# Local attention heads: scores from split queries and keys instead of float32 products, and an output projection whose first products wait row tile by row tile

## The reference, cut to what matters

```python
def swa_sinks_attention(q, k, v, sinks):       # q: 8 heads, k, v: 2 key heads, of 64 columns each
    ...                                        # keys of the block before and of the own block
    scores = jnp.einsum('bnqkgd,bnskd->bnkgqs', qb, kb).astype(jnp.float32) * scale
    scores = scores + alibi[None, None]
    scores = jnp.where(valid[None, :, None, None], scores, -jnp.inf)
    ...
    out = jnp.einsum('bnkgqs,bnskd->bnqkgd', p, vb)

mixed = jnp.concatenate([out_a.reshape(b, s, A_Q_W), out_b.reshape(b, s, B_W)], axis=-1)
x = x + jnp.einsum('bse,ed->bsd', mixed, w_out)
```

## Time and profile before

| | us |
|---|---|
| runs | 2723.07, 2725.77, 2720.76; median 2723.07 |
| profiled execution, its own time | 2724.15 |
| its span in the trace | 2722.3 |
| PE busy in the span | 2633.6 (97%) |
| DVE / ACT / POOL busy | 1837.4 / 1326.2 / 405.3 |
| end of block 2's projections | about 1700 to 1742 |
| attention of block 2 | about 1742 to 1987 |
| output projection of block 2 | about 1989 to 2045 and on |

### The profile page before, as it was taken

How to read it: one execution, slowest core, us unless ns; L and a number is a source line. 1 busy time by engine, 2 the same in 40 slices (tenths; PEclk the granted TensorE clock), 3 DMA queues, 4 the chain that set the end, 5 groups by cost and what they waited for, 6 DMA issues and landing times. The chain is left out here.

```text
span 2722.3 us, 37072 instructions
## 1 busy us (share of the span) xinstructions
PE 2633.6 (97%) x13612; PEld 2193.7 (81%) x13612; DVE 1837.4 (67%) x2469; ACT 1326.2 (49%) x1952; POOL 405.3 (15%) x359
## 2 busy tenths in 40 slices
PE   8999999999999899999999999899999999999999
PEld 7888876877788888888888788778888788888887
DVE  5761365457524888888888857566625875857878
ACT  3111243567432577877787422555533553525353
POOL 0222212100230122222221022300020000000000
PEclk9999999999999999999999999999999999999999
DMA  3115124311452699999999332100032616253451
GB/s 128 54 47 182 40 74 131 127 39 52 137 179 109 237 378 380 386 381 371 374 371 348 139 105 68 39 1 1 1 132 66 266 49 248 71 187 135 157 183 62
DMA packets 142456, 437.83 MB, mean 161 GB/s; under 512 B 23408, under 2 KB 45680, under 8 KB 110576
## 3 DMA queue, kind: packets, MB, share of 16 engines
q1 hardware_dynamic: 125312, 402.40, 41.0%
q0 software_dynamic: 10656, 20.99, 2.2%
q10 hardware_dynamic: 6352, 12.58, 1.2%
HBM read 387.68 MB, written 66.06 MB: 167 GB/s over the span
## 5 line engine op out<-in xcount | busy, mean ns | idle before, releaser
L2729 DVE TENSOR_TENSOR w_lo<-w_raw,w_hi 128x2048 fp32r<-128x2048 f32 x192 | 437.2, 2293 | 60.3 <-ACT w_hi L2663 59.3
L2663 ACT ACTIVATE w_hi<-w_raw 128x2048 fp32r<-128x2048 f32 x187 | 355.8, 1925 | 39.5 <-PE banks L2790 39.5
L3660 PE MATMUL banks<-b_parts,a_parts 128*128 128x512 f32 x1344 | 306.9, 390 | 6.3 <-DVE a_parts L3715 6.3
L3660 PE MATMUL banks<-a_parts,b_parts 128*128 128x512 f32 x1344 | 306.0, 389 | 2.3 <-DVE a_parts L3715 1.2
L3660 PEld LDWEIGHTS banks<-b_parts,a_parts 128*128 128x128 f32 x1344 | 251.8, 188 | 60.9 <-DVE a_parts L3715 8.8
L3660 PEld LDWEIGHTS banks<-a_parts,b_parts 128*128 128x128 f32 x1344 | 252.0, 188 | 55.2 <-DVE a_parts L3715 1.6
L3689 ACT ACTIVATE b_parts<-w_quarter 128x1024 fp32r<-128x1024 f32 x112 | 118.6, 1059 | 281.4 <-PE banks L3660 266.8
L766 POOL TENSOR_TENSOR w_lo<-w_raw,w_hi 128x512 fp32r<-128x512 f32 (+2 forms) x132 | 158.6, 1207 | 576.6 <-ACT w_hi L745 575.4
L745 ACT ACTIVATE w_hi<-w_raw 128x512 fp32r<-128x512 f32 (+2 forms) x132 | 73.9, 573 | 324.0 <-PE banks L824 306.0
L3709 DVE TENSOR_TENSOR b_parts<-w_quarter,b_parts 128x1024 fp32r<-128x1024 f32 x112 | 136.9, 1222 | 132.5 <-ACT b_parts L3689 132.5
L824 PE MATMUL banks<-w_hi,act_hi 128*128 128x512 f32 (+1 forms) x576 | 219.9, 382 | 6.0 <-POOL w_lo L766 3.7
(11 more groups left out here) (545 smaller groups left out, 5560.8 us busy)
## 6 DMA issues: line engine op xcount, KB each, us to landing
w_raw<-in_w SPq DMA_DIRECT2D x192, 1024.0 KB, 7.4
a_parts<-scratch_x_parts SPq DMA_DIRECT2D x42, 1024.0 KB, 4.8
w_raw<-in_w_in SPq DMA_DIRECT2D x80, 256.0 KB, 2.7
w_quarter<-in_w_up SPq DMA_DIRECT2D x16, 1024.0 KB, 6.9
w_quarter<-in_w_down SPq DMA_DIRECT2D x16, 1024.0 KB, 8.0
scratch_x_parts<-a_parts SPq DMA_DIRECT2D x14, 1024.0 KB, 5.1
scratch_gateT<-gate_staged SPq DMA_DIRECT2D x32, 256.0 KB, 2.2
gate<-scratch_gateT SPq DMA_DIRECT2D x32, 256.0 KB, 3.6
```

The costliest lines, as they stand in the source:

```text
L2663: act.activation(hi[c % SLOTS][:, :], raw[c % TILES][:, :], ACT.Copy).then_inc(hi_done, 1)
L2729: dve.tensor_tensor(lo[c % SLOTS][:, :], raw[c % TILES][:, :], hi[c % SLOTS][:, :].bitcast(F32), ALU.subtract).then_inc(lo_done, 1)
L3660: mm = pe.matmul(out, left, right, start=(start and n == 0), stop=(stop and n == 2))
```

## The change

1. **Scores of the local heads.** `qaT[g]` becomes fp32r with all 128 partitions in use: in the half that belongs to key head g the high part of the queries, in the other half their low part. `ka_hi[g]` holds the high part of key head g in both halves, `ka_lo` the low parts, each with three places ("slots") of 128 keys. A head's scores are two products: 128 rows (queries high and low against keys high) and 64 rows (queries high against keys low).
2. **Their preparation (step 2).** ACT makes four copies instead of three. DVE, which had no work there, makes four subtractions (two of 64x512, two of 64x128). POOL, which had none either, copies `ka_hi` from the one half into the other (2 copies) and, in even row tiles, also into slot 0 for the next row tile (5 more); each of its copies waits for the one before, the seventh for DVE too. PE's `wait_prepared` now waits for ACT, DVE and POOL in step 2 as well. In `project2_stage` the transposes after tile 30 wait for DVE's part of step 2, and DVE does that part after scaling four tiles of keys. Two memsets of `qaT` go.
3. **Output projection.** The four first weight tiles are loaded and split in the prelude (`Ring`): ACT puts their high parts between its sixteen copies, POOL makes the low parts meanwhile, and PE no longer waits for all sixteen parts of the rows but, for the first weight tile, for those of each row tile.

```diff
-    OF_ACT, OF_DVE = (2, 2, AKV + 1), (2, 2, 0)
+    OF_ACT, OF_DVE, OF_POOL = (2, 2, 4), (2, 2, 4), ((2, 2, 7), (2, 2, 2))
...
+    def pool_keys(self, pool, t):
+        n, done, k = self.own_slot(t), self.pool_upto[t, 2] - self.OF_POOL[t % 2][2], self.ka_hi
+        copies = [(k[0][self.BOTTOM, n, :], k[0][self.TOP, n, :]), (k[1][self.TOP, n, :], k[1][self.BOTTOM, n, :])]
+        if t % 2 == 0:
+            for r in (self.TOP, self.BOTTOM):
+                copies += [(k[0][r, 0, :], k[0][self.TOP, n, :]), (k[1][r, 0, :], k[1][self.BOTTOM, n, :])]
+            copies.append((self.ka_lo[:, 0, :], self.ka_lo[:, n, :]))
+        pool.wait_ge(self.prep_act, self.act_upto[t, 2])
+        for i, (dst, src) in enumerate(copies):
+            if done + i:
+                pool.wait_ge(self.prep_pool, done + i)
+            if i == 6:
+                pool.wait_ge(self.prep_dve, self.dve_upto[t, 2])
+            pool.tensor_copy(dst, src.bitcast(F32)).then_inc(self.prep_pool, 1)
...
+    def dve_local(self, dve, t, banks):
+        for b, bank in enumerate(banks):
+            dve.wait_ge(self.prep_act, self.act_upto[t, 2] - 2 + 2 * b)
+            n = self.own_slot(t)
+            for g, (own, other) in enumerate(((self.TOP, self.BOTTOM), (self.BOTTOM, self.TOP))):
+                if b == 0:
+                    lo, hi, src = self.v.qaT[g][other, :, :], self.v.qaT[g][own, :, :], self.blocks(bank, own)
+                else:
+                    lo, hi, src = self.ka_lo[own, n, :], self.ka_hi[g][own, n, :], bank[own, 0:P]
+                dve.tensor_tensor(lo, src, hi.bitcast(F32), ALU.subtract).then_inc(self.prep_dve, 1)
...
     def wait_prepared(self, pe, t, step):
         pe.wait_ge(self.prep_act, self.act_upto[t, step])
-        if self.dve_upto[t, step]:
-            pe.wait_ge(self.prep_dve, self.dve_upto[t, step])
-            pe.wait_ge(self.prep_pool, self.dve_upto[t, step])
+        pe.wait_ge(self.prep_dve, self.dve_upto[t, step])
+        pe.wait_ge(self.prep_pool, self.pool_upto[t, step])
...
-                30: [turn_first(0, 0, EARLY, (ops.columns_set, 1), (ops.prep_act, ops.act_upto[0, 2]))],
+                30: [turn_first(0, 0, EARLY, (ops.columns_set, 1), *after_both(0, 2))],
...
         scale(3, "kb", range(4))
+        ops.dve_part(dve, 0, 2, EARLY)
         ops.dve_part(dve, 0, 0, EARLY)
...
                     for a in range(HALF):
-                        mm = pe.matmul(pair[:, a * u.keys:(a + 1) * u.keys], qaT[u.g][:, a, :], kaT[:, (u.i + 1) * P - u.keys:(u.i + 1) * P],
-                                       start=True, stop=True)
+                        own = pair[:, a * u.keys:(a + 1) * u.keys]
+                        pe.matmul(own, qaT[u.g][:, a, :], ops.ka_hi[u.g][:, keys, :].rearrange("p n k -> p (n k)"), start=True, stop=False)
+                        mm = pe.matmul(own, qaT[u.g][rows_, a, :], ops.ka_lo[rows_, keys, :].rearrange("p n k -> p (n k)"), start=False, stop=True)
...
+    WEIGHTS_AFTER = {3: 0, 9: 1, 13: 2, 15: 3}
...
+    def row_waits(self, t):
+        return [(self.lo_done, max(2 * t + 2, 8 + t + 1))]
...
+        for n in range(self.COUNT):
+            act.wait_ge(self.turned, n + 1)
+            act.activation(self.part(v.act_hi, n), self.turned_rows(n), ACT.Copy).then_inc(self.hi_done, 1)
+            if n in self.WEIGHTS_AFTER:
+                i = self.WEIGHTS_AFTER[n]
+                act.wait_ge(self.ring.landed[i], 16)
+                act.activation(v.w_hi[:, i, :], v.w_raw[:, i, :], ACT.Copy).then_inc(self.ring.hi_done, 1)
...
+    tiles[0].rows_ready = {t: mixed.row_waits(t) for t in range(NT)}
```

More of the change, by code:

```diff
@@ L492, in __init__ @@
         self.first, self.last, self.b0 = first, last, b0
-        self.after = None
+        self.after, self.rows_ready = None, {}
         self.units = range(*rows_) if kind == "nat" else range(2 * (cols // P))
@@ L813, in _ @@
                         pe.wait_ge(free, freed[b])
+                    for s, count in tile.rows_ready.get(u, ()):
+                        pe.wait_ge(s, count)
                     if tile.kind == "nat":
@@ L1932, in _ @@
             keep_clock(pe, v, 7, 22)
[L1936 to L1991, removed]
-                mm = pe.transpose(v.bank[n % 8][:, c * P:(c + 1) * P], chunk(t, 4 * h + c), v.ident[:, :])
-            mm.then_inc(turned, 1)
-    return Prelude(sync, scalar, vector, tensor, [(hi_done, 2 * NT), (lo_done, 2 * NT)])
 BRANCH_W = 2 * P
@@ L3132, in f @@
             ops.pool_part(pool, t, step)
-            pool.wait_ge(ops.prep_pool, ops.dve_upto[t, step])
+            pool.wait_ge(ops.prep_pool, ops.pool_upto[t, step])
         return f
@@ L3208, in dve_program @@
         dve.wait_ge(attention_in, 48)
-        for g, r in enumerate((slice(HD, P), slice(0, HD))):
-            done(dve.memset(v.qaT[g][r, :, :], 0.0))
         done(dve.memset(v.R[:, :, :, :], 0.0))
@@ L3348, in _ @@
         def _(pool):
-            for t in range(2, NT):
-                pool.wait_ge(scored, starts[t - 1])
-                for step in range(2):
-                    ops.pool_part(pool, t, step)
+            for t, step in ops.SEQUENCE[5:]:
+                if step < 2:
+                    pool.wait_ge(scored, starts[t - 1])
+                ops.pool_part(pool, t, step)
         @block.vector
@@ L3500, in _, with __init__, part, turned_rows @@
             weigh(n_units - 1)
+class MixedRows:
+    COUNT = 2 * NT
+    WEIGHTS_AFTER = {3: 0, 9: 1, 13: 2, 15: 3}
+    def __init__(self, v, ring):
+        sem = v.sem
+        self.v, self.ring = v, ring
+        self.turned, self.hi_done, self.lo_done = sem("rows_turned"), sem("rows_hi"), sem("rows_lo")
+        self.ready = [(self.lo_done, self.COUNT)]
+    def part(self, x, n):
+        t, h = divmod(n, 2)
+        return x[:, 4 * h:4 * h + 4, t * P:(t + 1) * P]
+    def turned_rows(self, n):
+        return self.v.bank[n % 8].rearrange("p (c t) -> p c t", c=4)
+    def row_waits(self, t):
+        return [(self.lo_done, max(2 * t + 2, 8 + t + 1))]
+    def scalar(self, act):
+        v = self.v
+        for n in range(self.COUNT):
[5 more added lines that the diff above has]
+                act.activation(v.w_hi[:, i, :], v.w_raw[:, i, :], ACT.Copy).then_inc(self.ring.hi_done, 1)
+    def vector(self, dve):
+        v = self.v
+        for n in range(self.COUNT):
+            dve.wait_ge(self.hi_done, n + 1)
+            dve.tensor_tensor(self.part(v.act_lo, n), self.turned_rows(n), self.part(v.act_hi, n).bitcast(F32), ALU.subtract).then_inc(self.lo_done, 1)
+    def tensor(self, pe):
+        v = self.v
+        for n in range(self.COUNT):
+            t, h = divmod(n, 2)
+            if n >= 8:
+                pe.wait_ge(self.lo_done, n - 7)
+            for c in range(4):
+                mm = pe.transpose(v.bank[n % 8][:, c * P:(c + 1) * P], (v.out_a, v.out_b)[h][:, t, c * P:(c + 1) * P], v.ident[:, :])
+            mm.then_inc(self.turned, 1)
 def output2_stage(v):
     sem, d = v.sem, v.d
-    def mixers(t, k):
-        return (v.out_a if k < 4 else v.out_b)[:, t, k % 4 * P:(k % 4 + 1) * P]
     act = (v.act_hi, v.act_lo)
@@ L3512, in output2_stage, with load_w @@
     ready, free, x_in = sem("bank_ready"), sem("bank_free"), sem("x_in")
-    prelude = turn_rows(v, mixers)
+    ring = Ring(v)
+    mixed = MixedRows(v, ring)
+    tiles[0].rows_ready = {t: mixed.row_waits(t) for t in range(NT)}
+    def load_w(sp):
+        ring.load_first(sp, tiles)
     def load_x(sp):
```

39 lines of the change are left out of this document (26 added, 13 removed).

## The result

| | before | changed |
|---|---|---|
| median of the runs, us | 2722.84 (2720.76 to 2725.77) | 2771.37 (2767.72 to 2775.86) |
| ratio | | 1.0177, interval 1.0165 to 1.0190 |
| profiled execution, its own time | 2724.15 | 2769.5 |
| its span | 2722.3 | 2767.8 |

The changed kernel is slower by 48.5 us, where +5.1 was forecast and 2738 was the upper end. The profile after, in the order of the rows of before. First the page's busy time of the engines (answers to rows 1): PE is busy 36 us longer, so most of the loss isn't a wait.

The account below looks back on a forecast made before the run. The prediction took PE, busy for 97% of the span, as the bound; -10.0 + 12.2 + 2.6 - 4.2 + 4.5 = +5.1 us on 2723.07 gave 2728.2 us, range 2715 to 2738.

Parts of the forecast that it names:

- score products: Window units in the attention: two fp32r products a head at 0.12 us each, 0.83 us less in 12 units, -10.0 us.
- waits after step 2: Attention, row tiles 1 to 7: PE waits for DVE (odd) or POOL (even) at the shared banks, +12.2 us.
- waits ahead of preparations: PE's waits ahead of the transposes that a preparation starts with in the attention; the prediction had no term for them.
- projection stage: Step 2 of row tile 0: PE's transposes after tile 30 start 1.7 us late, and POOL's low part is later, +2.6 us.
- output projection: Its start: first weights are split earlier, so PE's first product comes 2.8 us sooner and a low-clock spell goes, -4.2 us.
- the clock: Attention and projection stage: three spells of low clock after the new waits, about 1.5 us each, +4.5 us.
- the products gain nothing: Rival on the score products: a 64-row load can't be hidden behind the product before, +15 us, 2738; chance 0.03.
- no faster DVE: Rival: six low-clock spells, and DVE's projection-stage scaling no faster while POOL stands, +12 us, 2735; chance 0.17.

Follow-up runs that it names:

- e2: The changed kernel with 128 rows instead of 64 in the second product of a head too: 2731.0 us.
- e1: The kernel before with the new order of the output projection alone: 2717.5 us.
- e8: The changed kernel with 64 rows in both products of a head, the queries' low parts left out of the first: 2737.7 us.
- e5: The changed kernel with a window unit's products ordered 128, 128, 64, 64 rows, so half as many changes of row count: 2739.0 us.
- e4: The changed kernel with its whole preparation and waits, but one float32 product a head, keys' low parts left out: 2740.3 us.
- e7: e2 with the shared banks waiting for ACT and DVE only and the weighing put ahead of that wait: 2713.6 us.
- e3: The kernel before with the two products a head (128 and 64 rows) from ACT's plain copies, no low parts or new waits: 2738.8 us.
- e6: The changed kernel with the shared banks waiting for ACT and DVE only and the weighing put ahead of that wait: 2743.3 us.
- e12: The changed kernel with six unread float32 products by the identity behind each window unit's scores from row tile 1 on: 2769.3 us.
- e11: The changed kernel with six unread float32 products by the identity in each wait behind step 2 from row tile 2 on: 2762.6 us.

## Why the prediction was wrong

The terms in the prediction's order; measured in the changed kernel unless said otherwise.

| term | forecast | measured |
|---|---|---|
| score products | -10.0 | +9.9 (14 units x 0.71), +2.2 in row tile 0 (0.25 a record for 0.11, two units) |
| waits after step 2 | +12.2 | +9.2 (12.2 less 3.0); in e2 +12.5 (15.5 less 3.0) |
| waits ahead of preparations | none | -1.8 (10.9 less 12.7) |
| projection stage | +2.6 | +2.4 (1.53 + 0.89) |
| output projection | -4.2 | -4.5 (7.4 for 11.9) and the spell behind it, -1.4; alone, in e1, -4.1 |
| the clock | +4.5 | +29.9 (78 less about 7 in the attention, x 0.42) |
| sum | +5.1 | +45.9; the spans differ by 45.5 |

**The step that failed first is the pace of the 64-row product** in "Gain of the score products": "the row of 84 rows (kb_hi) keeps the pace of 0.12, and I take that for 64 too". It comes at 0.31, above even the upper bound of 0.22 ("if nothing of it overlaps"), and so 8 records cost 0.71 us a unit more than float32 instead of 0.83 less. The rule of the Trainium skill that stood beside it (TensorE: Matmul & The Clock Gate, section LDWEIGHTS: the time of a load goes by its columns) isn't contradicted: e8's 64-row products do run at 0.12. Neither rule nor row speaks of the change from 128 rows to 64, and that is what costs (e5, e8). The rival "the products gain nothing" had what the loads show, a load that isn't hidden behind the product before, at a chance of 0.03 and with half the price; but the row count alone doesn't bring it (e8), the change does.

**The second is the size of the clock's term.** Three spells of 1.5 us were taken, all behind waits. In the changed kernel the spells are up to 17 us long, and 55 of the 78 us belong to spells that start in or right behind window units, with PE fully busy. The chain of argument held PE's idle time to be what to look at; the rows that it used come from a kernel in which no two such records came 0.31 us apart. With the pace restored, in e2, the clock's term is 13 us more at the lower level, 5.5 us, near the 4.5 of the forecast. That agreement is in part luck: 10 of the 13 us lie before 1790, with row tiles 1 and 2, while the forecast looked for the spells in the projection stage and from row tile 3 on.

**The clock's own cause is settled only in part.** Low clock by the kind of product and by the waits, in the profiled execution and, behind the stroke, over the whole kernel as the mean of all runs:

| products | waits short | waits of the change |
|---|---|---|
| float32 | 13 / 42 (before), 10 / 36 (e1) | 19 / 55 (e4) |
| 128 and 128 rows | 17 / 42 (e7) | 26 / 56 (e2) |
| 128 and 64 rows, alternating | 33 / 60 (e3), 40 / 66 (e6) | 78 / 112 (changed) |

Shown: the slow products raise it whether the waits are short or long, the longer waits raise it with each kind of product, and both together do by more than the sum (65 us, against 20 and 6; as the mean of all runs 70, against 18 and 13). Shown too: 64 rows in both products, at a pace of 0.12, have more of it (47 / 78, e8) than 128 rows in both at that pace and with like waits (26 / 56), and work behind the units lowers it (34 / 69, e12). Open: what in the slow products brings the clock down, and how the waits add to it. e6 shortens the waits but also moves the weighing, and e11, which fills them, lies between the two (87 in the mean, from 61 to 111).

**Right:** POOL's copies 0.34 apart; the waits after step 2, in row tiles 1, 3 and 5 1.4 to 1.8 us (1.0 to 1.7 were forecast) and put down to DVE, in 2, 4 and 6 1.8 to 2.9 (1.9 to 2.4) and ended by POOL; the two waits in the projection stage, and DVE's scaling there, whose operations take 0.69 to 0.78 us once POOL makes no low parts, so that the rival "no faster DVE" falls; the first product of the output projection 0.7 us behind the start of the last four transposes, at full clock. In row tile 7 the wait was missing: the unit of 2.5 us and the low clock had given DVE the time. Where the new products do run at the pace that was taken for them, in e2, a window unit takes 1.03 us instead of 0.96, since the first record takes 0.20, and the change costs 7.1 us in all where the sum had 5.1.

## What to carry to other kernels

Before products of half the rows are put between products of all rows, measure that very alternation: the pace of either alone doesn't tell. Widening the short product to the full rows, with an operand that adds nothing that counts, was worth 40 us here. Where a product gets faster but its operands need more work on other engines, first look at what that work will hold: here the order of two steps on PE, with the old float32 products, brought some 13 us (17.7 less the 4.1 of the output projection), more than the 10 that the new products were to bring.

## What the hardware showed that was not expected

- fp32r products of 256 columns: 0.12 us from one to the next for 128 after 128 rows, 64 after 64, 96 or 84 after 128 and back; 0.31 for 64 after 128 and for 128 after 64. With 128 columns 0.11 for 128 after 128, and 0.25 between 128 and 64. At such a change the weight load began together with its own product; elsewhere 0.11 to 0.12 us ahead of it.
- The granted clock fell to 0.50 for up to 17 us with PE 100% busy (13.60 of 13.60 us), from inside a run of products without idle time between them.
- POOL's copies of 64x128 came 0.34 us apart in the attention, but about 0.7 apart (4.24 us for six) beside DVE's scalings in the projection stage.
- Adding 20 us of products that nobody reads left the total time as it was (2769.3 and 2771.4 us), since 44 us at the lower clock went.
